# Two thirds of a linear-attention recurrence moved from the front of the kernel into its gathering blocks

## The reference

```
h  = RMSNorm(x) * (1 + scale1(c)) + shift1(c)
bg, cg, hin, q, k, v, r, ga, gb, alow = split(h @ w_in)
branch_a = (bg * short_conv(cg * hin)) @ w_proj_a
log_a = log_sigmoid(alow @ w_alpha + b_alpha) / 16
per head (4 heads, key 128, value 256), over tokens t:
    S_t = exp(log_a_t) * S_(t-1) + k_t v_t^T ;   o_t = q_t S_t
branch_b = (RMSNorm(o) * silu(r)) @ w_proj_b
x = x + g1 * RMSNorm((sigmoid(ga)*branch_a + sigmoid(gb)*branch_b) @ w_out)
h2 = RMSNorm(x) * (1 + scale2(c)) + shift2(c)
PEER: per token 8 heads pick 16 of 16384 experts by product keys:
    y = sum_k gate_k * gelu(u_k . h2) * v_k ;   x = x + g2 * RMSNorm(y)
```

## Time and profile before

| | us |
|---|---|
| median of 3 runs | 4568.08 (4566.28 to 4570.18) |
| span of the profiled execution | 4574.9 |
| PE busy in it | 3277.9 |
| DVE busy | 2488.2 |
| POOL busy | 1648.0 |
| ACT busy | 801.6 |
| gathering transfers, share of 16 DMA engines | 62.1% |
| other transfers from SP | 15.5% |

### The profile page before, as it was taken

The page is one execution under the profiler, slowest core; times in us unless marked ns, Lnnn a source line. Parts: engine busy times, 40 slices in busy tenths (PEclk is TensorE's granted clock), DMA queues, the critical chain, the costliest instruction groups (busy, mean ns, idle before and its releaser), DMA issues. The chain is left out here.

```text
span 4574.9 us, 46652 instructions
## 1 busy us (share of the span) xinstructions
PE 3277.9 (72%) x15679; PEld 1680.7 (37%) x15679; DVE 2488.2 (54%) x7735; ACT 801.6 (18%) x1284; POOL 1648.0 (36%) x1379
## 2 busy tenths in 40 slices
PE   8899997736389666686678676667666667666666
PEld 2798896636056441341145344124210101111110
DVE  2245553126764445577755454557786555555554
ACT  2232333232014113110013211211000100000000
POOL 1211104523245444442345444344333333333332
PEclk9999998968589886897789888678765666666666
DMA  7211103533789889898889898999899999999998
GB/s 278 73 58 49 39 29 131 171 118 111 274 334 407 338 354 379 345 384 341 337 348 405 345 393 356 383 375 362 354 387 360 415 404 405 409 412 409 414 411 346
DMA packets 243430, 1400.14 MB, mean 306 GB/s; under 512 B 30661, under 2 KB 47685, under 8 KB 100986
## 3 DMA queue, kind: packets, MB, share of 16 engines
q0 software_dynamic: 156672, 1140.92, 62.1%
q1 hardware_dynamic: 86522, 256.22, 15.5%
HBM read 1345.59 MB, written 51.43 MB: 305 GB/s over the span
## 5 line engine op out<-in xcount | busy, mean ns | idle before, releaser
L1057 DVE CUSTOM_DVE_ANT_0 peer_uv<-peer_uv,all_PS 128x512 f32<-128x512 f32 x2176 | 1435.3, 685 | 1164.2 <-DMA peer_uv<-in_uv,peer_idx 804.8
L996 PE MATMUL all_PS<-peer_hT,peer_sel 96*128 96x512 bf16 x2176 | 1002.4, 484 | 1027.4 <-DVE peer_halves L1057 842.5
L979 POOL DMA_INDIRECT peer_uv<-in_uv,peer_idx x1088 | 1043.4, 959 | 1756.9 <-PE all_PS L1015 1379.6
L996 PEld LDWEIGHTS all_PS<-peer_hT,peer_sel 96*128 96x128 bf16 x2176 | 203.0, 102 | 2002.9 <-DVE peer_halves L1057 1632.6
L1015 PE MATMUL all_PS<-peer_uv,peer_zw 128*32 128x512 f32 x4352 | 871.7, 849 | 2.4 <-DVE peer_zw L1077 2.4
L867 POOL TENSOR_TENSOR flow_w_lo<-flow_w,flow_w_hi 128x1024 fp32r<-128x1024 f32 (+1 forms) x204 | 460.4, 2261 | 456.5 <-ACT flow_w_hi L860 455.9
L1031 ACT ACTIVATE peer_ge<-peer_pre 128x4 f32<-128x4 f32 x272 | 55.7, 205 | 2109.7 <-DVE peer_pre L1063 2109.6
L887 PE MATMUL all_PS<-mix_h_hi,flow_w_hi 128*128 128x384 f32 (+1 forms) x672 | 279.6, 416 | 32.2 <-POOL flow_w_lo L867 31.8
L860 ACT ACTIVATE flow_w_hi<-flow_w 128x1024 fp32r<-128x1024 f32 (+1 forms) x204 | 203.5, 1003 | 359.2 <-PE all_PS L889 110.7
L888 PE MATMUL all_PS<-mix_h_lo,flow_w_hi 128*128 128x384 f32 (+1 forms) x672 | 226.3, 337 | 0.0
L889 PE MATMUL all_PS<-mix_h_hi,flow_w_lo 128*128 128x384 f32 (+1 forms) x672 | 226.1, 336 | 0.0
(11 more groups left out here) (290 smaller groups left out, 4670.4 us busy)
## 6 DMA issues: line engine op xcount, KB each, us to landing
cond_w<-in_w_ada SPq DMA_DIRECT2D x12, 2048.0 KB, 8.1
flow_w<-in_w_gate_ab SPq DMA_DIRECT2D x48, 512.0 KB, 7.1
flow_w<-in_w_query SPq DMA_DIRECT2D x48, 512.0 KB, 7.7
flow_w<-in_w_conv SPq DMA_DIRECT2D x36, 512.0 KB, 4.5
peer_uv<-in_uv,peer_idx POOLq DMA_INDIRECT x1088, 10.4
gla_w<-in_w_heads SPq DMA_DIRECT2D x24, 512.0 KB, 4.4
flow_w<-in_w_proj_b SPq DMA_DIRECT2D x24, 512.0 KB, 7.8
flow_w<-in_w_out SPq DMA_DIRECT2D x24, 512.0 KB, 8.4
```

The source lines that it names most:

```text
L979: self.nc.gpsimd.indirect_dma_start(out=self.uv[:, n % self.NUV, :], out_offset=None, in_=self.A["uv"], in_offset=bass.IndirectOffsetOnAxi ...
L996: nc.tensor.matmul(PS[:, f, :], self.sel[:, c:c + 1].broadcast_to([3 * GR, P]), self.hT[:, g % self.NH, f * 512:(f + 1) * 512], start=True ...
L1057: nc.vector.tensor_tensor_reduce(part, part, PS[:, f, :], 1.0, 0.0, ALU.mult, ALU.add, self.halves[:, d, f, e:e + 1]).then_inc(M["dotted"], 1)
```

## The change

`heads_phase` still projects all nine tiles, but runs the recurrence of the first three only (tiles 0, 1 and the samples). It stores q, k, v, g and the gated r of the other six tiles, and the state S, to DRAM (`inputs`, `put`). Its 48 r slots now stand as 10, 13, 13, 0, 12. The sums of squares, the root and the final products cover 320 columns instead of 1088, except r times its Sigmoid.

A new stage `recur_phase` opens the second and the third block, before `mix_phase`. It works through 12 units, tile by tile and head by head within a tile. Each unit loads q, k, v, g and r, does the recurrence for one tile and head, normalises and stores the result. Between its steps it does gathering turns like the other stages. The shares become seven: 100 for the new stage, the six old ones behind it. The index and gate buffers of the gathering hold six tiles instead of nine, in rotation.

```diff
-        FILL = [KD] + [KD // 2] * (NT - 1) + [0, KD]
+        FILL = [10, 13, 13, 0, 12]
+            def inputs(i):
+                sp.wait_ge(M["q_out"], 3 * i + 3)
+                sp.dma_start(later("qkv", i)[:, :, :, 0:P], tiled(q[:, FT:T])).then_inc(M["qk_saved"], 16)
...
+                sp.wait_ge(M["v_out"], NT * i + NT)
+                sp.dma_start(later("qkv", i)[:, :, :, 2 * P:4 * P], v[:, 2:NT - 1, None, :]).then_inc(M["v_saved"], 16)
             def put(i):
...
-                for part in PARTS:
-                    sp.dma_start(A["ob"][part.index, ...], o[...]).then_inc(M["ob_saved"], 16)
+                for e in range(2):
+                    sp.dma_start(later("rs", i)[:, :, :, e * P:(e + 1) * P], tiled(r[:, e, FT:T])).then_inc(M["r_saved"], 16)
+                sp.dma_start(A["ob"][0, :, bass.ds(i, 1), :, 0:FT], o[:, None, :, :]).then_inc(M["ob_saved"], 16)
-                for t, n, kind in tiles:
+                for j, t, n, kind in here:
...
-SHARES = (94, 50, 38, 42, 90, 100)
+SHARES = (100, 94, 50, 38, 42, 90, 100)
...
+                    if part.index:
+                        recur_phase(nc, A, G, part, gat, marks[0], marks[1])
```

The heart of the new stage, PE's, ACT's and DVE's queue for a unit m (waits cut where they are plain):

```diff
+def recur_phase(nc, A, G, part, gat, lo, hi):
+        NU = H * nt
+        turns = Turns(lo, hi, 3 * NU)
+        bankE, bankR = PS[:, FRONT, :], PS[:, FRONT + 3, :]
...                                                     # PE
+                    gat.spread(pe, turns.upto(3 * m))
+                    pe.wait_ge(M["qk"], 3 * m + 3)
+                    nc.tensor.transpose(bankE[:, 384:512], K[:, m % 2, LV, :], G["ident"][:, :]).then_inc(M["t_mm"], 1)
+                    for l in range(LV + 1):
+                        last = nc.tensor.matmul(PS[:, FRONT + 1 + l // 4, ...], lhs, rhs, start=True, stop=True)
+                    gat.spread(pe, turns.upto(3 * m + 1))
+                    exponents(m + 2, 0)
+                    results(m - 1)
+                    gat.spread(pe, turns.upto(3 * m + 2))
+                    exponents(m + 2, 1)      # each waits for the Exp of the one before: one bank
+                    state(m - 1)
+                    exponents(m + 2, 2)
+                    squares(m - 1)
...                                                     # ACT
+                    gat.gelu(act, turns.upto(3 * m)); copy kT; gat.gelu(act, turns.upto(3 * m + 1))
+                    exps(m + 2, 0); copy o; Square of o; gat.gelu(act, turns.upto(3 * m + 2))
+                    exps(m + 2, 1); exps(m + 2, 2); make_high(m + 3); Ln and Exp of the root
...                                                     # DVE
+                    gat.dots(dve, turns.upto(3 * m))
+                    masked scores, two halvings, sT; finish(m - 2)
+                    gat.dots(dve, turns.upto(3 * m + 1)); gat.dots(dve, turns.upto(3 * m + 2))
+                    new state S; decay(m + 2); make_low(m + 3)
```

More of the change, by code:

```diff
@@ L417, in heads_phase @@
         tiles = [(t, rows(t), 0 if t < NT - 1 else 1) for t in range(NT)]
-        assert NT % 2
+        here = [(j, t, rows(t), 0 if t < NT - 1 else 1) for j, t in enumerate(ORDER[0:NFRONT])]
+        assert NFRONT % 2 and here[-1][1] == NT - 1
         PIECES = [(e, t0, n) for e in range(2) for t0, n in TB]
-        FILL = [KD] + [KD // 2] * (NT - 1) + [0, KD]
+        FILL = [10, 13, 13, 0, 12]
         filled = [sum(FILL[:j]) for j in range(len(FILL) + 1)]
@@ L557, in exponents, with results @@
                         mask = SUMS[kind][0:n, 3 * b:3 * b + 3, 0:n]
-                        nc.tensor.matmul(out, g_hi[0:n, t, :], mask, start=True, stop=False)
-                        last = nc.tensor.matmul(out, g_lo[0:n, t, :], mask, start=False, stop=True)
+                        nc.tensor.matmul(out, g_hi[0:n, j, :], mask, start=True, stop=False)
+                        last = nc.tensor.matmul(out, g_lo[0:n, j, :], mask, start=False, stop=True)
                     last.then_inc(M["e_mm"], 1)
[L562 to L568, removed]
+                def results(j, t, n, kind):
+                    if j >= 1:
+                        pe.wait_ge(M["st_out"], NSF * i + j)
+                        pe.wait_ge(M["o_out"], NFRONT * i + j)
+                    for e in range(2) if j >= 1 else ():
+                        nc.tensor.matmul(PS[:, 6, e * P:e * P + n], S[:, e * P:(e + 1) * P], Qc[:, j % 3, 0:n],
@@ L701, in _ @@
-                output(*tiles[NT - 1])
-                emptied(NT + 1)
-                act.wait_ge(M["o_out"], NT * i + NT)
-                nc.scalar.activation(q[:, :], o[:, 0, :], ACT.Square)
-                nc.scalar.activation(k[:, :], o[:, 1, :], ACT.Square).then_inc(M["sq_ready"], 1)
+                for j, t, n, kind in here:
+                    if j >= 1:
+                        output(*here[j - 1])
+                        emptied(j)
+                        act.wait_ge(M["st_mm"], NSF * i + j)
+                    act.wait_ge(M["t_mm"], NFRONT * i + j + 1)
+                    nc.scalar.activation(kT[0:n, :], PS[0:n, 5, 0:DK], ACT.Copy).then_inc(M["t_out"], 1)
+                    if j + 2 < NFRONT:
+                        exps(*here[j + 2])
@@ L733, in _ @@
                 dve.wait_ge(M["act_own"], 4 * i + 4)
[L734 to L736 removed]
+                for n, t in ((P, slice(0, NT - 1)), (TAIL, slice(NT - 1, NT))):
+                    gg, low_z = soft[0:n, t], least[0:n, t]
                     nc.vector.scalar_tensor_tensor(out=gg, in0=gg, scalar=-1.0 / TAU, in1=low_z, op0=ALU.mult,
```

528 lines of the change are left out of this document (407 added, 121 removed).

## The result

The changed kernel takes 4699.42 us (median of 4 runs, 4693.87 to 4718.41) against 4569.13 us (4566.28 to 4573.15) for the kernel before: ratio 1.0285, interval 1.026 to 1.031, slower. The profiled executions have spans of 4692.1 and 4574.9 us, 117.2 us apart. The prediction said +99 us.

What follows compares the result with a forecast made beforehand. PE bounds the heads' stretch; transfers nearly bound the second and third block. Front −108, old stages −273 and new stages +480 gave +99 us, 4667 us on the median; range 4572 to 4745 us, to hold 8 in 10.

Steps and rivals of the forecast that it cites:

- The new stages: Second and third block: 195 and 237 us plus 24 us each for start and end, 480 us together.
- rival 3: New stages: a unit's serial chain sets the pace, DVE idling; 564 us there, total +183 us, 4751 us; chance 0.14.
- The front: Heads' stretch: shorter by 27 us a head, 108 us for four heads, as PE work leaves it.
- Rival 4: Front: time not given back, waiting for stores or a load, 15 us a head; 4727 us; chance 0.05.
- The old stages' relief: Six old stages of the second and third block: 2.08 us saved per token moved out, 273 us together.
- the floor's 2.66: Last block's gathering at DMA share 1.01: 2.66 us a token, taken as the most a moved token could save.
- My upper bound, 348 us: Old stages: the most their relief could be, each moved token saving 2.66 us.
- My ratio of 1.12: New stages: time over the transfers' demand, 1.12 in the second block and 1.08 in the third.
- the transfers' demand: New stages: tokens at 2.66 us plus 22 us of other transfers, 174 us in the second block, 219 in the third.
- Start and end: Each new stage: barrier, loads, first exponents and decays, last results and state stores, 24 us a stage.
- Rival 1: New stages hidden under the transfers, 405 us, each moved token saving 2.66 us: −51 us, 4517 us; chance 0.15.
- The rule on table sets: ACT in the new stage: the skill page says Ln then Exp needs one table load; the trace shows two.

Runs made afterwards that it cites:

- experiment 1: The changed kernel without the new stages and the later blocks' recurrence, old shares, front as changed: 4466.99 us, ratio 0.976 to the kernel before.
- experiment 4: The changed kernel with share 160 instead of 100 for the new stage, 82 and 107 tokens in place of 57 and 74: 4700.67 us, ratio 1.027.
- experiment 5: The changed kernel with plain copies for the root's Ln and Exp in the new stage, so without their table loads: 4704.88 us, ratio 1.027.
- experiments 8 to 10: The changed kernel with one token group a unit, then exponents, results and state product ahead of it, then eight tokens at stage start: 4631.88, 4615.18, 4599.08 us.
- experiment 2: The changed kernel with the new stages doing only their tokens' gathering, the later blocks' recurrence left out: 4486.73 us, ratio 0.980.
- experiment 10: The changed kernel with one token group a unit, exponents, results and state product ahead of it, eight tokens before the first unit: 4599.08 us, ratio 1.006.

## Why the prediction was right

The sign and the size held: +99 us foretold, +117 in the profile and +130 between the medians. That the size held was luck in part: two of its terms were off by 90 and 103 us, in opposite directions. Of the signs that I had named, the heads' stretch (471 us, PE over 90% busy) and mix (202 us) came out. The new stages did not: 267 and 316 us against at most 240 and 280, DMA share 0.71 and 0.74 against 0.8, DVE busy 59 and 57% of them against over 70. What I had named as rival 3's sign, DVE idle before the decays and the masked scores, is there.

- **The front.** −108 foretold, −102.5 measured, 25.6 us a head; the step counted from the timeline alone, 25.8 us, was nearer than the 27 that I took. Rival 4 is out: PE is busy 431 of 471 us, and experiment 1 keeps the whole gain.
- **The old stages' relief was mis-sized.** I took 2.08 us a token and −273 us; it is −363 us for 131 tokens, 2.77 each. That goes against both of its arguments, that the floor's 2.66 bounds it and that above 2.08 is the less likely side. The 2.08 came from comparing the second block with the third, which is no experiment with tokens: with 310 tokens the third block's old stages take 1035.0 us, with 296 the second's took 1042.2. Something that is not its tokens makes the second block 46 us longer (1042.2 against 1035.0 − 14 × 2.77 = 996.2); what, I did not try. That the relief gets smaller as tokens leave did hold: the next 58 tokens of experiment 4 gave back 128.7 us, 2.22 each. My upper bound, 348 us, was a little too low.
- **The new stages were mis-sized the other way.** 480 us foretold, 583 measured. My ratio of 1.12 over the transfers' demand (1.08 in the third block) came from keys and pick; here three token groups and as many pieces of recurrence alternate in a unit. Start and end were sized right: barrier, start and end are 11, 24 and 21 us at DMA shares 0.55, 0.52 and 0.53, which loses 26 us of transfers, and I had taken 24. What is left, 267 − 26 = 241 us, is 1.39 times the demand of 174; in the third block (316 − 26) / 219 = 1.32. The step that failed is that ratio.
- **Rivals.** Rival 1 asked for DMA share 0.93 in the new stages; they have 0.71 and 0.74. Yet its first half was true: each moved token gave back the floor's pace. It failed on the recurrence's cost, which it had hidden. Rival 3's size, 564 us, was the best figure for the new stages, and its total of +183 us was too high only because it was put beside my low relief. Its mechanism was half right: the scores at the low clock and the waits for the Exp are in the trace, but the bank's chain is worth 29 us, the clock at the scores at most some 10 and the root's table loads nothing; three groups to one are worth 61 to 68 us.
- **The rule on table sets.** The trace after agrees with the trace of before: Ln and the Exp behind it have a load each, of 1.28 us. My reading of the earlier trace rows, that each next instruction starts as its load ends, holds for the Exp and the Sigmoid; the Ln's load ran at 286.36 and the Ln at 293.28, once PE's sums were there, so that load was hidden. As experiment 5 shows, the difference between that and the one load of the page "ScalarE: Activation LUTs" of the Trainium skill (section "Table sets: the hidden batching unit") would have changed no term of the sum.

Why it is slower can then be said in two steps. The two prices are measured, the reasons beside them are read from the traces. In the front a unit stood beside projections that kept PE busy and left DVE idle for 302 of 574 us, and cost 4.3 us. In the blocks it stands beside the gathering, which wants DVE, PE and the transfers in turn, and cost 8.9 us. Some 100 us of the 213 come from the order and from where the first tokens stand (experiments 8 to 10: 213 to 112 us). The rest, 4.7 us a unit, is about what the front had saved, and the tokens' own stages cost 20 us (experiment 2), so even the best order stays 26 us above the kernel before. Why no order went below that is open. DVE's own work in a unit, 83% of 7.7 us or 6.4 us, added to 1.4 us a token, is 12 × 6.4 + 57 × 1.4 = 157 us of the 174 that the transfers need, and DVE is busy 157 us in experiment 10's new 2 (227.1 us). Of its 70 idle us there 19.7 stand before a spread, 17.6 before the scores, 13.3 at the start before the gates' low part and 6.3 before a root. I did not find which of them could still go, and no run with less of DVE's work or fewer transfers tells which of the two holds the rest.

## What to carry to other kernels

Room in each engine's busy share does not make work free in a stretch that transfers nearly bound: by the sums DVE needed 159 us and the transfers 174 in the first new stage, and it took 267, in the best order 221 to 227. Where two streams share in-order queues, try them in few large groups before anything else: 24 units with one group instead of three were 61 to 68 us faster with the same instructions, some 50 of them by the grouping itself. Putting one stream's cross-engine steps ahead of the group took out two waits, brought part of them back as a third, and was worth some 20 us more. And measure the give-back of a moved item with the item alone (an empty stage), not by comparing two stages that differ in other ways.

## What I had not expected of the hardware

- With tokens in it the units' stretch had a mean granted clock of 0.78, without them 1.00, although PE was busy 72 and 74% of either. In these two stretches the share of busy time does not tell the clock.
- ACT's load fell by a third in experiment 5 and the time did not move by its uncertainty: at 0.43 of the stretch ACT had room for the root's table loads.
- Tokens alone ran at 0.98 DMA share with the clock at 0.67: there the low clock left the transfers next to full.
